# The last three of 256 row gathers, each issued in two parts (2 rows and 126 rows)

## The chip, the core and the metric

One core of a Trainium2 chip runs the whole program. The metric is device time in microseconds (us) of one execution; the kernel before was timed in three runs, and their median counts. Beside it stands one profiled execution, from whose trace all rows here come.

## What is computed

The reference is a chain of transformer blocks on 256 tokens of width 1024 (two layers with feed-forward parts and attention, then convolution mixers and a cross attention). Its last part is what this change touches. For each token, 8 heads choose 16 experts each out of 16384; each chosen expert is a row of `u` and a row of `v`:

```python
u_sel = jnp.take(u, ec, axis=0)
act = gelu(jnp.einsum('chkd,cd->chk', u_sel, hc)) * gc
v_sel = jnp.take(v, ec, axis=0)
return jnp.einsum('chk,chkd->cd', act, v_sel)
```

The result is added to the token's vector, a final RMS norm follows, and the 256 x 1024 output is written.

## The kernel before, in words

The tokens are two tiles (t = 0 and 1) of 128, one token to a partition. A head choice is a column of 128 indices, one per token, so there are 2 x 128 = 256 columns n (`N_ROWS`), gathered in order. `u` and `v` stand side by side in one table, `peer_uv`, so that one gathered row is 2048 floats (8 KB), and one gather of 128 rows is 1 MB.

**POOL** (`gather`, line 786, its DMA at line 806) issues one indirect DMA for each n: row p of the table named by `IDX[p, n]` goes to partition p of `row_pair[n % 16]`. There are 16 such buffers (`ROW_SLOTS`), so from n = 16 on it first waits until the row pair of n - 16 has been used (line 805). The DMA counts `row_loaded[n % 16]` up by 16.

**DVE** (loop from line 2656) does for each n, in this order: `dot(n)` (line 2600: wait for the landing, then product with the token and row sum, into `DOT`); at each fourth n `coefficients` of the four columns before (line 2607: gelu value times gate); and for two of every four columns (n % 4 = 1 or 3) `weighted` (line 2619: coefficient times the v half, added to `XTOK`). It also runs the search for the indices of later heads, whose last step writes 16 columns of `IDX` (line 2580, counted by `idx_ready`). At the end the columns are taken in smaller groups: 252 and 253 together, then 254, then 255 (`COEFS`). The last steps of DVE are thus: dot(252), coefficients of 248 to 251, dot(253), weighted(249), dot(254), weighted(251), coefficients of 252 and 253, dot(255), coefficients of 254, weighted(253), coefficients of 255, weighted(255), `total` (line 2626), `finish` (line 2635).

**ACT** makes the gelu of each group (line 1903) and, for the other two of every four columns (n % 4 = 0 or 2), a diagonal matrix of the coefficients (line 1890). **PE** multiplies that diagonal with the v half (line 1331, two halves of 512 columns, sums kept in PSUM) and ends with a closing product (line 1336); `total` adds PSUM to `XTOK`.

**SP** loads the weights of all earlier parts, then the last gain (line 650), and then waits for the four pieces of the output, `yo_ready`, and writes each (lines 651 to 654): two pieces for token tile 0, two for tile 1.

`mod_ring` is a reused area whose parts hold `IDX`, `DOT`, `CF` and the like in this last stage; the profile shows them all under the name mod_ring.

Of the kernel before, what the change touches and what calls it, by code (L numbers as in the profile page):

```python
# [10 lines left out]
U32 = mybir.dt.uint32  # L11
# [5 lines left out]
P = 128  # L17
# [155 lines left out]
ROW_SLOTS = 16  # L173
# [4 lines left out]
N_ROWS = TT * SLOTS_PER_TILE  # L178
N_HEADS = TT * PH
AHEAD = 3  # L180


def row_use(n):
# [61 lines left out]
def build_program(nc, a, out):  # L245
    ctx = ExitStack()
    with ctx:
# [3 lines left out]
        def sem(name):  # L251
            return ctx.enter_context(nc.semaphore(name))
# [15 lines left out]
        def place(name, at_, n, dt=F32, parts=P):  # L268
            assert at_ + n <= ARENA
            return nc.alloc_sbuf_tensor_at(name, [parts, n], dt, offset=arena_at + 4 * at_)  # L270
# [14 lines left out]
        row_pair = [place(f"row_pair{k}", at_, 2 * D) for k, at_ in enumerate(row_areas)]  # L285
# [112 lines left out]
        def mr(n, a0=None, dt=None):  # L398
            v = mod_ring[:, at_mr[0]:at_mr[0] + n]
            at_mr[0] += n  # L400
            if dt is not None:
                v = v.bitcast(dt)
            return v if a0 is None else v.rearrange("p (a b) -> p a b", a=a0)
# [16 lines left out]
        IDX = mr(256, None, U32)  # L420
# [3 lines left out]
        GS = mr(16)  # L424
        YS = mr(4)
        RT = mr(TT)
        assert at_mr[0] <= 2 * TILE

        ps = ctx.enter_context(nc.psum_tensor("ps", [P, 8, 512], F32))
# [142 lines left out]
        gate_diff = sem("gate_diff")  # L572
        gate_exp = sem("gate_exp")
        idx_ready = sem("idx_ready")
        dots_done = sem("dots_done")
        gelu_ready = sem("gelu_ready")
        cf_ready = sem("cf_ready")
        diag_ready = sem("diag_ready")
        row_loaded = [sem(f"row_loaded{s}") for s in range(ROW_SLOTS)]
# [11 lines left out]
        @block.sync  # L591
        def _(sp):
            sp.dma_start(table[0:NB, :], a["rel_bias"]).then_inc(small_loaded, 16)
            sp.dma_start(onehot[:, :], a["onehot"]).then_inc(small_loaded, 16)
            sp.dma_start(lamp[:, :], a["a_lambda"].partition_broadcast(P).rearrange("q a n -> q (a n)")).then_inc(small_loaded, 16)
            sp.dma_start(fgate_b[:, :], a["fgate_b"]).then_inc(small_loaded, 16)
            sp.dma_start(prm[:, :], a["prm"]).then_inc(prm_loaded, 16)
            sp.dma_start(c_row, a["c_row"].partition_broadcast(P).rearrange("q a n -> q (a n)")).then_inc(c_row_loaded, 16)
            sp.dma_start(X[:, :, :], a["xT"]).then_inc(x_loaded, 16)

            sp.wait_ge(mod_eaten, 2)

            def tiles(name, t0=0, n=None, i=None):

                ln = LIN[name]
                for t in range(t0, t0 + (ln.tiles if n is None else n)):
                    g = ln.tile0 + t
                    if g >= RING:

                        low_wait(sp, g - RING, i)  # L610
                    if name[:2] == "a_" and name != "a_o":
                        sp.dma_start(slot(raw, g), a[name[:3]][int(name[3])]).then_inc(w_loaded[g % RING], 16)
                        continue
                    if name in ("x_k0", "x_k1"):
                        src = a["x_k"][t + 2 * (name == "x_k1")]
                        sp.dma_start(slot(raw, g), src).then_inc(w_loaded[g % RING], 16)
                        continue
                    src = a[name][t] if i is None else a[name][bass.ds(i * BODY + t, 1)].rearrange("a p f -> (a p) f")
                    sp.dma_start(slot(raw, g), src).then_inc(w_loaded[g % RING], 16)

            def ffn(w_in, w_out):
                tiles(w_in, 0, RING)
                with sp.Fori(0, 3) as i:
                    tiles(w_in, RING, BODY, i)
                tiles(w_in, 21, 1)
                tiles(w_out)

            ffn("f00_in", "f00_out")
            for kind, t in A_ORDER:
                tiles(f"a_{kind}{t}")  # L630
            tiles("a_o")
            ffn("f01_in", "f01_out")
            tiles("s_k")
            tiles("s_v")
            ffn("f10_in", "f10_out")
            tiles("b_q")
            tiles("b_o")
            sp.wait_ge(mods_ready, summed(ADA_TILES // 2 - 1))
            sp.dma_start(subk[:, :, :], a["subkT"]).then_inc(sub_loaded, 16)
            sp.dma_start(MEM, a["memT"]).then_inc(mem_loaded, 16)  # L640
            ffn("f11_in", "f11_out")
            for name in ("x_k0", "mix_a", "mix_g", "x_k1", "x_v", "mix_b", "sc_out", "cf_out", "mix_out", "x_q", "x_o"):
                tiles(name)
            tiles("pq", 0, 3)
            sp.wait_ge(units_done, LIN["x_o"].unit_end)
            for t in range(TT):
                sp.dma_start(HTOK[:, t, :], a["norm_peer_row"].partition_broadcast(P).rearrange("q a n -> q (a n)")
                             ).then_inc(gpeer_loaded, 16)
            tiles("pq", 3, 5)
            sp.dma_start(gfin, a["final_norm_g"].partition_broadcast(P).rearrange("q a n -> q (a n)")).then_inc(gfin_loaded, 16)  # L650
            for t in range(TT):
                for c in range(2):
                    sp.wait_ge(yo_ready, 2 * t + c + 1)
                    sp.dma_start(out[t][:, c * 512:(c + 1) * 512], XTOK[:, t, c * 512:(c + 1) * 512]).then_inc(out_written, 16)
            sp.wait_ge(out_written, 32 * TT)
# [3 lines left out]
        def _(pool):  # L659
# [126 lines left out]
            def gather(n):  # L786

                if n % TK == 0:
                    pool.wait_ge(idx_ready, n // TK + 1)
                if n == 1:  # L790
                    pool.wait_ge(el_ready, ESET["attX"] + DC)
                if n == 3:
                    pool.wait_ge(tok_turned, 4)
                if n in (4, 5, 8):

                    pool.wait_ge(low["v"], LOW[pq.tile0 + {4: 5, 5: 6, 8: 7}[n]][1])
                if n in (6, 9, 11):

                    pool.wait_ge(units_done, CHUNK_UNIT[pq.chunk0 + 2 * {6: 5, 9: 6, 11: 7}[n] + 1])
                if n == 14:  # L800

                    pool.wait_ge(sub_scores, TT * PH)
                if n >= ROW_SLOTS:
                    e, used = row_use(n - ROW_SLOTS)
                    pool.wait_ge(rows_used[e], used)
                pool.indirect_dma_start(  # L806
                    out=row_pair[n % ROW_SLOTS][:, :], out_offset=None, in_=a["peer_uv"],
                    in_offset=bass.IndirectOffsetOnAxis(ap=IDX[:, n:n + 1], axis=0),
                ).then_inc(row_loaded[n % ROW_SLOTS], 16)

            for n in range(N_ROWS):
# [529 lines left out]
        def _(act):  # L1341
# [506 lines left out]
            act.wait_ge(sumsq_ready, RANK[N_PEER] + 1)  # L1848
            f(RT, ps_token, ACT.Sqrt, scale=1.0 / D, bias=eps[:, :]).then_inc(token_root, 1)

            def sub_copies(h):

                for t in range(TT):
                    act.wait_ge(sub_scores, 2 * h + t + 1)
                    f(S[t][:, 2 * h:2 * h + 2, :].rearrange("p a n -> p (a n)"), ps[:, SUBKEY_BANK[t], 0:2 * NK],
                      ACT.Copy, scale=RT[:, t:t + 1]).then_inc(s_ready, 1)

# [40 lines left out]

            for g in range(AHEAD):
                gates_exp(g)  # L1900
            for j, (first, last) in enumerate(COEFS):
# [4 lines left out]
                if last == SLOTS_PER_TILE + ROW_SLOTS:  # L1906
                    length(0)
                g = last // TK - 1 + AHEAD
                if last % TK == 0 and g < N_HEADS:
# [5 lines left out]
        def _(dve):  # L1915
# [572 lines left out]
            dve.wait_ge(token_root, 1)  # L2488
            v.reciprocal(RT, RT).then_inc(token_scale, 1)

# [105 lines left out]

            def dot(n):

                dve.wait_ge(row_loaded[n % ROW_SLOTS], 16 * (n // ROW_SLOTS + 1))
                v.scalar_tensor_tensor(row_u(n), row_u(n), 1.0, HTOK[:, n // SLOTS_PER_TILE, :], ALU.mult, ALU.mult,  # L2600
                                       accum_out=DOT[:, n:n + 1]).then_inc(dots_done, 1)

# [37 lines left out]
            splits = iter(range(pq + 3, pq + 8))  # L2640
            for g in range(AHEAD - 1):
                for _ in head_best(0, g):
# [9 lines left out]
            for t in range(TT):  # L2652
                v.scalar_tensor_tensor(HTOK[:, t, :], XTOK[:, t, :], RT[:, t:t + 1], HTOK[:, t, :], ALU.mult, ALU.mult
                                       ).then_inc(htok_ready, 1)
            dve.wait_ge(htok_ready, TT)
            for n in range(N_ROWS):
                head, k = n // TK, n % TK
                if k == 0:
                    later = search(head + AHEAD) if head + AHEAD < N_HEADS else iter(())
                dot(n)  # L2660
                if n == BATCH - 1:
                    for _ in search(AHEAD - 1):
                        pass
# [119 lines left out]
```

## Time and profile before

| | |
|---|---|
| three timed runs | 2128.24, 2128.47, 2130.43 us; median 2128.47 |
| the profiled execution | 2122.55 us, of which 2120.7 us from the first to the last instruction (its span) |
| busy share of the span | PE 84%, DVE 82%, ACT 40%, POOL 26% |
| bytes | 606.26 MB over the span, 270.57 MB of them on the software queue of POOL |
| first and last gather issued | 1452.2 and 2080.8 us from the span's start |

Times in rows are us from the span's start. A row of the timeline gives start, duration, engine, line, operation, operands and, in brackets, the idle time of the engine just before it and what ended it. The DMA share is the mean busy share of the core's 16 DMA engines: one engine busy alone shows as 0.06. PEclk is the granted clock of TensorE as a share of 2.4 GHz.

### The profile page before, as it was taken

What the parts mean: (1) busy time and instruction counts of PE and PEld (TensorE: products, weight loads), DVE (VectorE), ACT (ScalarE), POOL (GpSimd) and SP (SyncE); (2) the same over time, 40 slices, a digit from 0 to 9 for tenths busy, and PEclk for the clock granted to TensorE, in tenths of its full rate; (3) what the DMA queues carried; (4) which work ended last, traced back from release to release, by engine and by line L of the source; (5) the groups of instructions that cost most, each with busy time, mean ns of one, the idle gap of its engine ahead of it and who ended that gap; (6) DMA issues with size and microseconds to landing.
All of it is one profiled execution on the core that took longest, in us unless ns stands there. A gap on an engine that the chain in (4) does not pass through costs nothing.

```text
span 2120.7 us, 30890 instructions
## 1 busy us (share of the span) xinstructions
PE 1780.8 (84%) x11460; PEld 1499.9 (71%) x11460; DVE 1729.6 (82%) x2997; ACT 858.0 (40%) x1336; POOL 559.9 (26%) x487
## 2 busy tenths in 40 slices
PE   5999898999999998899999999999655665554655
PEld 4999798999999987899899999989222222211221
DVE  5888777888988887754689997758999989998877
ACT  3443466544454446644545445554212111111101
POOL 0111002111001113111320002422555554545441
PEclk7999999999999998999999999999888777778677
DMA  7889733688868884254545444428999999999996
GB/s 319 318 312 370 306 121 140 250 317 297 293 247 321 302 328 165 100 200 172 182 166 195 173 177 169 178 100 319 412 422 422 422 423 422 422 423 422 422 423 262
DMA packets 88784, 606.26 MB, mean 286 GB/s; under 512 B 9763, under 2 KB 11059, under 8 KB 21468
## 3 DMA queue, kind: packets, MB, share of 16 engines
q1 hardware_dynamic: 37708, 245.03, 31.6%
q0 software_dynamic: 37040, 270.57, 30.7%
q10 hardware_dynamic: 13920, 89.15, 10.5%
q8 instruction: 69, 1.13, 0.2%
q14 instruction: 47, 0.39, 0.0%
HBM read 601.53 MB, written 3.18 MB: 285 GB/s over the span
## 4 chain that ended last, share of the span: by engine, by line
PE 22%; DVE 18%; DMA 15%; issue 3%; ACT 2%; POOL 1%; DVEq 0%; POOLq 0%; ACTq 0%
DMA row_pair<-in_peer_uv,mod_ring 15%; PE ps L834 12%; DVE row_pair L2600 4%; DVE w_lo L1923 3%; DVE XTOK L2619 3%; PE ps L865 2%; PE ps L1331 2%; DVE work L2370 2%; PE ps L966 2%; DVE SQ L2370 2%; PE ps L967 1%; POOL row_pair L806 1%; PE ps L897 1%; PE ps L1027 0%; ACT w_hi L1353 0%
## 5 line engine op out<-in xcount | busy, mean ns | idle before, releaser
L1923 DVE TENSOR_TENSOR w_lo<-raw,w_hi 128x2048 fp32r<-128x2048 f32 (+1 forms) x248 | 528.2, 2134 | 183.1 <-ACT w_hi L1353 182.4
L1331 PE MATMUL ps<-row_pair,diag 128*128 128x512 f32 x512 | 356.2, 860 | 265.9 <-ACT diag L1890 265.9
L1353 ACT ACTIVATE w_hi<-raw 128x2048 fp32r<-128x2048 f32 (+1 forms) x248 | 440.2, 1776 | 214.5 <-PE ps L834 70.1
L1331 PEld LDWEIGHTS ps<-row_pair,diag 128*128 128x128 f32 x512 | 136.1, 279 | 485.3 <-ACT diag L1890 321.2
L834 PE MATMUL ps<-HH,w_hi 128*128 128x256 f32 x1584 | 443.9, 280 | 0.5 <-DVE w_lo L1923 0.5
L834 PE MATMUL ps<-HH,w_lo 128*128 128x256 f32 x1584 | 442.2, 279 | 0.0
L834 PE MATMUL ps<-HL,w_hi 128*128 128x256 f32 x1584 | 441.1, 278 | 0.0
L806 POOL DMA_INDIRECT row_pair<-in_peer_uv,mod_ring x256 | 329.3, 1286 | 321.6 <-PE ps L1331 220.4
L2600 DVE SCALAR_TENSOR_TENSOR row_pair<-row_pair,HTOK 128x1024 f32<-128x1024 f32 x256 | 311.5, 1218 | 62.6 <-DMA row_pair<-in_peer_uv,mod_ring 60.1
L834 PEld LDWEIGHTS ps<-HL,w_hi 128*128 128x128 f32 x1584 | 297.6, 188 | 0.7 <-issue 0.7
L834 PEld LDWEIGHTS ps<-HH,w_hi 128*128 128x128 f32 x1584 | 296.4, 187 | 2.1 <-DVE w_lo L1923 1.2
L834 PEld LDWEIGHTS ps<-HH,w_lo 128*128 128x128 f32 x1584 | 296.6, 187 | 0.0
L966 PE MATMUL ps<-GUHL,w_hi 128*128 128x512 f32 x704 | 247.2, 395 | 2.1 <-DVE w_lo L1923 2.1
L720 POOL TENSOR_TENSOR GUHL<-work,GUHL 128x256 f32 (+1 forms) x88 | 79.1, 899 | 537.7 <-ACT GUHL L1473 497.1
L1940 DVE SCALAR_TENSOR_TENSOR mod_ring<-mod_ring,mod_acc 128x1024 f32<-128x1024 f32 x144 | 192.7, 1375 | 19.8 <-DMA mod_ring<-in_ada 19.1
L967 PE MATMUL ps<-GUHL,w_lo 128*128 128x256 f32 x704 | 197.4, 280 | 0.0
L1903 ACT ACTIVATE mod_ring<-mod_ring 128x4 f32<-128x4 f32 (+1 forms) x66 | 13.5, 205 | 397.8 <-DVE row_pair L2600 397.8
L834 PE MATMUL ps<-EH,w_hi 128*128 128x256 f32 x560 | 159.6, 285 | 5.6 <-POOL EL L693 2.8
L2619 DVE SCALAR_TENSOR_TENSOR XTOK<-row_pair,mod_ring,XTOK 128x1024 f32<-128x1024 f32 x126 | 161.2, 1279 | 0.0
L834 PE MATMUL ps<-EL,w_hi 128*128 128x256 f32 x560 | 158.9, 284 | 0.0
L834 PE MATMUL ps<-EH,w_lo 128*128 128x256 f32 x560 | 158.0, 282 | 0.0
L966 PEld LDWEIGHTS ps<-GUHL,w_hi 128*128 128x128 f32 x704 | 132.0, 187 | 33.7 <-DVE w_lo L1923 3.1
(338 smaller groups left out, 3004.3 us busy)
## 6 DMA issues: line engine op xcount, KB each, us to landing
raw<-in_f_in SPq DMA_DIRECT2D x88, 1024.0 KB, 4.9
mod_ring<-in_ada ACTq DMA_DIRECT2D x74, 1024.0 KB, 7.2
raw<-in_f_out SPq DMA_DIRECT2D x64, 704.0 KB, 5.5
raw<-in_mix_a SPq DMA_DIRECT2D x16, 1024.0 KB, 4.8
raw<-in_mix_g SPq DMA_DIRECT2D x8, 1024.0 KB, 4.7
raw<-in_pq SPq DMA_DIRECT2D x8, 1024.0 KB, 5.0
first<-in_ada ACTq DMA_DIRECT2D x4, 1024.0 KB, 13.0
raw<-in_a_q SPq DMA_DIRECT2D x4, 1024.0 KB, 5.1
```

What stands on the lines that cost most here:

```text
L720: nc.gpsimd.tensor_tensor(lo, graw[:, j % 2, :], f32(hi), ALU.subtract).then_inc(hidden_lo, 1)
L806: pool.indirect_dma_start(out=row_pair[n % ROW_SLOTS][:, :], out_offset=None, in_=a["peer_uv"], in_offset=bass.IndirectOffsetOnAxis(ap=IDX ...
L834: ins = mm(out_, ops[1] if left else ops[0], ops[0] if left else ops[1], start=(first and k == k0 and n == 0), stop=(last and k == k1 - 1 ...
L966: mm(pair, w[0][:, kk, :], GUHL[:, :, k * SEQ:(k + 1) * SEQ], start=(k == 0), stop=False)
L967: last = mm(ps[:, BANK[q], 0:SEQ], w[1][:, kk, :], GUH[:, k, :], start=False, stop=(k == FC - 1))
L1331: last = mm(ps[:, 2 * t + c, :], diag[:, d, :], row_v(k)[:, c * 512:(c + 1) * 512], start=False, stop=False)
L1353: f(slot(w_hi, g), slot(raw, g), ACT.Copy).then_inc(hi_ready, 1)
L1923: v.tensor_tensor(slot(w_lo, g), slot(raw, g), f32(slot(w_hi, g)), ALU.subtract).then_inc(low["v"], 1)
L1940: ins = v.scalar_tensor_tensor(w[:, j, :], w[:, j, :], 1.0, c_row, ALU.mult, ALU.mult, accum_out=mod_dot[:, n // 2 % 2, m:m + 1])
L2370: ins = v.scalar_tensor_tensor(dst, x, w31, dst, ALU.mult, ALU.add)
L2600: v.scalar_tensor_tensor(row_u(n), row_u(n), 1.0, HTOK[:, n // SLOTS_PER_TILE, :], ALU.mult, ALU.mult, accum_out=DOT[:, n:n + 1]).then_inc ...
L2619: ins = v.scalar_tensor_tensor(y, row_v(n), CF[:, n:n + 1], y, ALU.mult, ALU.add)
```

## The change

The gathers of n = 253, 254 and 255 become two indirect DMAs each, the first for rows 0 and 1, the second for rows 2 to 127. Because an index column is given from partition 0 on, the indices of the second part are first copied down two partitions, into `part_idx`, by a DMA of SP once the last index is there. Each part counts the buffer's semaphore up by 16, and `dot` waits for one 16 more at these three columns. The copy stands in SP's program ahead of the waits for the output.

```diff
+PARTED = 3
+FIRST_PART = 2
+def row_loads(n):
+    return 2 if n >= N_ROWS - PARTED else 1
...
+        part_idx = mr(PARTED, None, U32)
...
+            sp.wait_ge(idx_ready, N_HEADS)
+            sp.dma_start(part_idx[0:P - FIRST_PART, :], IDX[FIRST_PART:P, N_ROWS - PARTED:N_ROWS]).then_inc(part_idx_loaded, 16)
             for t in range(TT):
                 for c in range(2):
                     sp.wait_ge(yo_ready, 2 * t + c + 1)
...
+                whole = row_loads(n) == 1
+                rows = P if whole else FIRST_PART
                 pool.indirect_dma_start(
-                    out=row_pair[n % ROW_SLOTS][:, :], out_offset=None, in_=a["peer_uv"],
-                    in_offset=bass.IndirectOffsetOnAxis(ap=IDX[:, n:n + 1], axis=0),
+                    out=row_pair[n % ROW_SLOTS][0:rows, :], out_offset=None, in_=a["peer_uv"],
+                    in_offset=bass.IndirectOffsetOnAxis(ap=IDX[0:rows, n:n + 1], axis=0),
+                ).then_inc(row_loaded[n % ROW_SLOTS], 16)
+                if whole:
+                    return
+                k = n - (N_ROWS - PARTED)
+                if k == 0:
+                    pool.wait_ge(part_idx_loaded, 16)
+                pool.indirect_dma_start(
+                    out=row_pair[n % ROW_SLOTS][rows:P, :], out_offset=None, in_=a["peer_uv"],
+                    in_offset=bass.IndirectOffsetOnAxis(ap=part_idx[0:P - rows, k:k + 1], axis=0),
                 ).then_inc(row_loaded[n % ROW_SLOTS], 16)
...
-                dve.wait_ge(row_loaded[n % ROW_SLOTS], 16 * (n // ROW_SLOTS + 1))
+                dve.wait_ge(row_loaded[n % ROW_SLOTS], 16 * (n // ROW_SLOTS + row_loads(n)))
```

## Rows read from the trace of the kernel before

**Rows 1.** The chain that ended last, its last DMA piece: start, length, what.

```profile
2079.59 27.11 DMA row_pair<-in_peer_uv,mod_ring
```

**Rows 2.** Windows of the gather stage and its end; columns in the first line.

```profile
core 0: us, PE busy (x) PEld busy (x) DVE busy (x) ACT busy (x) POOL busy (x), PEclk, DMA share, GB/s
2000.00:2050.00 50.00, 28.88 (x40) 11.12 (x40) 37.74 (x60) 4.50 (x15) 22.56 (x20) 0.76 1.01 422
...
2098.00:2099.00 1.00, 1.00 (x3) 0.19 (x1) 1.00 (x3) 0.00 (x0) 0.00 (x0) 1.00 0.57 238
...
2100.00:2100.50 0.50, 0.00 (x0) 0.00 (x0) 0.50 (x2) 0.00 (x0) 0.00 (x0) 1.00 0.12 49
2100.50:2101.00 0.50, 0.00 (x0) 0.00 (x0) 0.07 (x2) 0.20 (x1) 0.00 (x0) 1.00 0.04 16
...
2107.00:2108.00 1.00, 1.00 (x2) 0.34 (x1) 1.00 (x3) 0.00 (x0) 0.00 (x0) 0.50 0.06 25
...
2108.50:2109.00 0.50, 0.50 (x3) 0.14 (x1) 0.50 (x1) 0.00 (x0) 0.00 (x0) 1.00 0.00 0
```

**Rows 3.** DMA packets of 2101.4 to 2108.5: queue: packets, MB, share of 16 engines.

```profile
DMA packets 25, 0.19 MB, mean 27 GB/s; under 512 B 2, under 2 KB 2, under 8 KB 2
...
q0 software_dynamic: 25, 0.19, 6.3%
```

**Rows 4.** Timeline of the last columns, from dot(252) to the total of tile 1.

```profile
2101.80 1.23 DVE L2600 SCALAR_TENSOR_TENSOR row_pair<-row_pair,HTOK 128x1024 f32<-128x1024 f32 x1 [1.23 <-DMA row_pair<-in_peer_uv,mod_ring]
...
2102.95 0.16 DVE L2607 TENSOR_TENSOR mod_ring<-mod_ring 128x4 f32<-128x4 f32 x1
...
2103.59 5.88 PE L1331 MATMUL ps<-row_pair,diag 128*128 128x512 f32 x8 [4.52 <-ACT diag L1890]
2104.26 1.23 DVE L2600 SCALAR_TENSOR_TENSOR row_pair<-row_pair,HTOK 128x1024 f32<-128x1024 f32 x1 [1.15 <-DMA row_pair<-in_peer_uv,mod_ring]
...
2106.72 1.23 DVE L2600 SCALAR_TENSOR_TENSOR row_pair<-row_pair,HTOK 128x1024 f32<-128x1024 f32 x1
...
2109.07 0.15 DVE L2607 TENSOR_TENSOR mod_ring<-mod_ring 128x2 f32<-128x2 f32 x1
2109.18 1.23 DVE L2600 SCALAR_TENSOR_TENSOR row_pair<-row_pair,HTOK 128x1024 f32<-128x1024 f32 x1
2109.26 0.40 ACT L1890 ACTIVATE diag<-ident,mod_ring 128x128 f32<-128x128 f32 x1 [3.53 <-DVE mod_ring L2607]
...
2109.72 3.70 PE L1331 MATMUL ps<-row_pair,diag 128*128 128x512 f32 x8 [0.24 <-ACT diag L1890]
...
2111.80 1.28 DVE L2619 SCALAR_TENSOR_TENSOR XTOK<-row_pair,mod_ring,XTOK 128x1024 f32<-128x1024 f32 x1
...
2113.90 1.22 DVE L2626 TENSOR_TENSOR XTOK<-XTOK,ps 128x1024 f32<-128x1024 f32 x1 [0.82 <-PE ps L1336]
```

**Rows 5.** POOL: all its gathers (ns min/median/max), and gathers 253 and 255.

```profile
L806 POOL DMA_INDIRECT row_pair<-in_peer_uv,mod_ring x256: 934/1249/2792, 1452.2 to 2080.8; - x128
...
2078.35 0.94 POOL L806 DMA_INDIRECT row_pair<-in_peer_uv,mod_ring  x1 [0.31 <-issue]
...
2080.84 0.94 POOL L806 DMA_INDIRECT row_pair<-in_peer_uv,mod_ring  x1 [0.30 <-issue]
```

**Rows 6.** The index writes of DVE and the output DMAs of SP, first and last start.

```profile
L2580 DVE SCALAR_TENSOR_TENSOR mod_ring<-mod_ring x16: 158/161/175, 1451.8 to 1982.7; 128x16 uint32<-128x16 f32 x16
...
L654 SPq DMA_DIRECT2D out<-XTOK x4: 332/338/348, 1851.6 to 2118.3; - x4
```

**Rows 7.** Packet prices: 1.70 to 1.96 us (all small), and 2117 to 2121 (output).

```profile
DMA packets 48, 0.00 MB, mean 4 GB/s; under 512 B 48, under 2 KB 48, under 8 KB 48
...
q1 hardware_dynamic: 48, 0.00, 8.8%
...
q1 hardware_dynamic: 288, 0.52, 33.9%
```

**Rows 8.** PE's group of eight matmuls one before the last three.

```profile
2093.68 5.40 PE L1331 MATMUL ps<-row_pair,diag 128*128 128x512 f32 x8 [4.54 <-ACT diag L1890]
```

More of the change, by code:

```diff
@@ L574, in build_program @@
         idx_ready = sem("idx_ready")
+        part_idx_loaded = sem("part_idx_loaded")
         dots_done = sem("dots_done")
```

## The prediction

> **What bounds the kernel now.** I read the chain of waits first, from its end backwards. Its last long piece is a gather's transfer, 27.11 us from 2079.59, so it lands at 2106.70 [rows 1]; that is the time at which dot(254) begins. What comes after it is compute of the last columns. So the end is set by the row transfers until the last few us.
>
> Next the windows [rows 2]. Through the stage the DMA share is 1.01 at 422 GB/s: all 16 engines are busy, each at 422 / 16 = 26.4 GB/s, which is 0.31 us for a row of 8,192 bytes and 2.48 us for an equal share of 8 of a gather's 128 rows. But the engines don't stop together. The share falls to 0.57 in 2098 to 2099, to 0.12 (two engines) in 2100 to 2100.5, and then stays at 0.06, one engine, with nothing new started after 2108.5. The packets of that tail prove it [rows 3]: from 2101.4 to 2108.5 only 25 packets are left, 2 of them small (completions) and 23 rows, with 6.3% of 16 engines, which is one engine without a gap at 0.31 us a row. Three gathers have 3 x 8 = 24 rows for one engine. So **one engine is three gathers behind**, fifteen are done by about 2100.7, and columns 253, 254 and 255 wait for the lone one.
>
> Last the timeline [rows 4]. dot(252) waited 1.23 us for its landing at 2101.80, dot(253) 1.15 us at 2104.26, one share of 2.48 later. dot(254) and dot(255) start with no idle time shown: DVE needs nearly as long as the transfer. On the other branch PE works from 2103.59 to 2109.47 on the diagonals of columns 248 and 250 (eight matmuls, 5.88 us), idles 0.24, and takes 3.70 us for the eight of 252 and 254. The total at 2113.90 waited for PE. The granted clock explains 5.88 against 3.70: 0.50 (1.2 GHz) in 2107 to 2108, still in the first group, and 1.00 (2.4 GHz) from 2108.5 on [rows 2].
>
> **The parts of the change.**
>
> *Where the rows go.* No row shows a gather of 2 or 126 rows. Whole gathers go in equal shares of 8. Equal shares of 126 can't be on 16 engines; 14 engines with 9 rows are the nearest (9 engines with 14, 7 with 18, and so on down to one with 126). Two rows make one each on two engines. If the lone engine is one of the two that the 14 leave, it has 1 row in place of 8 in each of three gathers, 21 fewer: 21 x 0.31 = 6.5 us off its tail. The others get 3 more, 0.93 us. Bounds for the lone engine: from no row at all (all 7.4 us of its 24 rows gone) to all 128 of each. I take one row per gather, the case nearest to the equal shares that the rows show in which its load changes. The Trainium skill ("DMA: Bandwidth & Descriptors", section "Why a DMA increments its semaphore by 16 and not by 1") says that a DMA runs on the largest number of engines up to 16 that divides its rows, on POOL's path consecutive ones from a cursor that goes round. By that rule the parts take 2 and 14 engines and bring the cursor back to the same place, so the same two engines are spared three times; the sum is the same by it. No run here shows it.
>
> *POOL.* Three gathers become six. Gather 253 starts at 2078.35 and the next follow at 0.94 + 0.30 us [rows 5], so the sixth part is out by 2078.35 + 6 x 1.25 = 2085.9. The earliest engine stops about 2098 and so reaches column 253 about 7.4 us before, 2090.6. Were each part 2.79 us (the longest gather), the sixth would be out at 2096.9; that delays only engines that have several us to spare. Cost 0; nothing stands behind these on POOL.
>
> *SP and the index copy.* The last index is written at 1982.7, and SP's output DMAs were issued from 1851.6 to 2118.3 [rows 6]. The two for token tile 0, ready at 1851.6, now stand behind the wait for the last index and go out 131 us later, still 135 before the last two. Nothing else waits for them, and their 0.52 MB (1.2 us of all engines) lie in the same full DMA stage either way: 0. POOL's new wait asks for a copy issued near 1983; at 2079 it is long there. The copy itself is 126 runs of 12 bytes, 8 or 9 per engine, taken out of the saturated stage, so it delays the lone engine, dot(252) and all behind. Bounds: 48 small packets took 8.8% of 16 x 0.26 us, 7.6 ns each; 256 output packets of 2 KB took 33.9% of 16 x 4 us, 84 ns each [rows 7]. That is 0.07 to 0.76 us; 12 bytes are nearest to the small ones, so +0.07.
>
> *The tail with the lone engine relieved.* Column 252 is whole and still lands at 2101.80. Then three single rows, 0.93: the lone engine lands 255 by 2102.8. The others stop at 2100.7 + 0.93 = 2101.6 and land 0.5 later. So nothing is awaited after dot(252). DVE: coefficients at 2102.95, and dot(253) 0.11 later (as 2109.07 to 2109.18 in [rows 4]), 2103.06 in place of 2104.26: 1.20 earlier. The next coefficients come at 2107.87 in place of 2109.07, the diagonal of 252 is ready about 2108.5. But PE is in its slow group until 2109.47. It then starts at once: 2109.47 + 3.70 = 2113.17 in place of 2113.42. **Gain 0.24 us**, PE's idle time. DVE's own last product would end at 2113.08 - 1.20 = 2111.88, before PE. What is late next is thus PE at 1.2 GHz. An earlier group of eight took 5.40 us [rows 8]; then the gain would be 0.72. The bound is DVE's 1.20.
>
> **Sum.** -0.24 + 0.07 = -0.17 us. The profiled execution took 2122.55 us (span 2120.7 and 1.85 around it), so 2122.4; the median of the timed runs is 5.92 above it, and I carry the difference over: **2128.3 us**. A measurement of this kernel tells about 0.2% (4.26 us) from no change, since the three runs alone spread by 2.19.
>
> **Rivals.**
>
> A. *The lone engine is among the 14.* It gets 9 rows: columns 253, 254 and 255 land 0.31, 0.62 and 0.93 later. dot(254), which began at its landing, moves by 0.60; so do the coefficients, the diagonal and PE's last group. DVE ends at 2113.08 + 0.93 = 2114.0, before PE's 2114.5. With the copy +0.67: 2129.1. For it: no row tells which engine is the lone one. The Trainium skill (the same page, section "Latency and other measured facts") says that engines 7 and 15 are usually slower; a cursor at 0 would spare 0 and 1, and this rival would hold. The trace shows one lone engine, not a pair, and no number, so this rule bears little.
>
> B. *Few engines take the 126 rows* (the rival that ends slower). Place: the landing of column 255. With r rows an engine in each gather an engine that now stops at 2100.7 stops at 2100.7 + (r - 8) x 0.93. It passes today's 2108.7 from r = 17, seven engines or fewer, and costs 4.3 us more from r = 22: 8 + (8.0 + 4.3) / 0.93. With three engines (r = 42) it is 24 us, 2152; with one, 110 - 8 = 102 us, 2230. Against it: whole gathers use all engines.
>
> C. *The parts are dealt as before*, about 8 rows an engine, the last one less: the change does not do what it says. The lone engine keeps its tail, +0.07 to +0.4: 2128.7.
>
> **Chances.** Relieved 0.50, A 0.38, B 0.05, C 0.07. Between the first two the trace can't choose; I put relief ahead because the whole tail sits on one engine, and it matters little: both lie within 0.04%. Within 0.2% are the first, A and C, 0.95 together, less 0.06 for medians of three runs that differ by themselves and for a stage that runs otherwise without the profiler (5.92 us lie between): **same 0.89**. Of the rest, B past r = 22 gives 0.03, scatter 0.04 up and 0.04 down: **slower 0.07, faster 0.04**. Range: from the bound -1.20 to A with the dearest copy, 0.60 + 0.76 = +1.36, widened by half the spread of the runs, 1.1, on either side: 2126.2 to 2130.9.
>
> **What would show it.** Right: after about 2102.5 no DMA work but output; dot(253) idle-free near 2103.1 after a dot(252) that still waits; PE's last two groups without a gap. Wrong: a share of 0.06 that lasts to 2109 or beyond (A or C), a share of 0.2 to 0.5 past 2109 (B). The forecast falls if the slow matmul group is shorter or PE's clock is up earlier, which frees up to 1.20, or if dot(252) itself lands elsewhere.

## The result and the profile after

The changed kernel takes 2136.88 us in the median of six runs (2135.74 to 2138.34), the kernel before 2129.14 us beside it (six runs, 2128.24 to 2130.43). The ratio is 1.0036 with a 95% interval of 1.0025 to 1.0046: **slower by 7.7 us**, outside the forecast range and beyond the 0.2% that the forecast took as the line of a difference.

The profiled execution of the change took 2137.66 us, with a span of 2135.8. It stood 7.7 us behind the profiled execution of before already at the first `dot` (1480.8 and 1473.1), long before anything changed can act. So I compare one stretch of both traces, from the start of dot(244) to the end of the span: 2120.7 - 2081.95 = 38.7 us before, 2135.8 - 2090.08 = 45.7 us after. The two lines of dot(244), before and after:

```profile
2081.95 1.23 DVE L2600 SCALAR_TENSOR_TENSOR row_pair<-row_pair,HTOK 128x1024 f32<-128x1024 f32 x1 [2.22 <-DMA row_pair<-in_peer_uv,mod_ring]
...
2090.08 1.23 DVE L2622 SCALAR_TENSOR_TENSOR row_pair<-row_pair,HTOK 128x1024 f32<-128x1024 f32 x1 [2.21 <-DMA row_pair<-in_peer_uv,mod_ring]
```

The difference, 7.0 us, agrees with the medians. The index copy and the moved output lie ahead of that stretch; run 1 below times them alone.

First the windows of the changed kernel, as in [rows 2] (columns: window, its length, busy us and instructions of PE, PEld, DVE, ACT, POOL, then PEclk, DMA share, GB/s).

```profile
2050.00:2100.00 50.00, 28.83 (x40) 10.94 (x40) 36.91 (x58) 4.50 (x15) 21.43 (x20) 0.73 1.02 415
2100.00:2102.00 2.00, 0.00 (x0) 0.00 (x0) 0.70 (x1) 0.00 (x0) 0.00 (x0) 1.00 0.95 225
...
2110.00:2112.00 2.00, 0.00 (x0) 0.00 (x0) 2.00 (x3) 0.00 (x0) 0.00 (x0) 1.00 0.90 229
2112.00:2114.00 2.00, 0.00 (x0) 0.00 (x0) 0.49 (x2) 0.00 (x0) 0.00 (x0) 0.85 0.34 94
...
2118.00:2120.00 2.00, 1.88 (x3) 0.84 (x4) 0.95 (x1) 0.36 (x2) 0.00 (x0) 0.50 0.06 25
```

The point is in the last two columns. In the windows from 2100 to 2112 the engines are nearly as busy as before (share 0.86 to 0.95, here the first and the last), yet they move 189 to 233 GB/s, about half of 422. A busy share alone would have hidden this. The tail at 0.06, one engine, is still there after 2114.

The packets of that stretch (number, MB, mean rate; then the queue's packets, MB and share of 16 engines) give the price of a row.

```profile
DMA packets 479, 2.81 MB, mean 216 GB/s; under 512 B 136, under 2 KB 136, under 8 KB 136
...
q0 software_dynamic: 479, 2.81, 91.1%
```

This is 2099 to 2112, 13 us. 479 - 136 = 343 rows of 8 KB took 0.911 x 16 x 13 = 189 us of engine time: **0.55 us a row in place of 0.31** [rows 3]. Read one by one in the packed trace, none of these 343 rows took under 0.35 us, on any engine.

The timeline of the changed kernel, the rows that answer to [rows 4] (dot is now line 2622, the diagonal product 1353, the total 2648):

```profile
2097.53 1.23 DVE L2622 SCALAR_TENSOR_TENSOR row_pair<-row_pair,HTOK 128x1024 f32<-128x1024 f32 x1
...
2101.30 1.23 DVE L2622 SCALAR_TENSOR_TENSOR row_pair<-row_pair,HTOK 128x1024 f32<-128x1024 f32 x1 [2.53 <-DMA row_pair<-in_peer_uv,mod_ring]
...
2105.66 1.22 DVE L2622 SCALAR_TENSOR_TENSOR row_pair<-row_pair,HTOK 128x1024 f32<-128x1024 f32 x1 [3.06 <-DMA row_pair<-in_peer_uv,mod_ring]
...
2113.91 1.23 DVE L2622 SCALAR_TENSOR_TENSOR row_pair<-row_pair,HTOK 128x1024 f32<-128x1024 f32 x1 [1.51 <-DMA row_pair<-in_peer_uv,mod_ring]
...
2116.33 1.23 DVE L2622 SCALAR_TENSOR_TENSOR row_pair<-row_pair,HTOK 128x1024 f32<-128x1024 f32 x1 [1.18 <-DMA row_pair<-in_peer_uv,mod_ring]
...
2119.05 1.23 DVE L2622 SCALAR_TENSOR_TENSOR row_pair<-row_pair,HTOK 128x1024 f32<-128x1024 f32 x1 [1.42 <-DMA row_pair<-in_peer_uv,mod_ring]
...
2124.61 1.22 DVE L2622 SCALAR_TENSOR_TENSOR row_pair<-row_pair,HTOK 128x1024 f32<-128x1024 f32 x1 [0.26 <-DMA row_pair<-in_peer_uv,mod_ring]
...
2129.01 1.22 DVE L2648 TENSOR_TENSOR XTOK<-XTOK,ps 128x1024 f32<-128x1024 f32 x1 [0.51 <-PE ps L1358]
```

These are the dots of 247, 248, 249, 251, 252, 253 and 255, and the total. The same two dots before, 247 and 251:

```profile
2089.41 1.23 DVE L2600 SCALAR_TENSOR_TENSOR row_pair<-row_pair,HTOK 128x1024 f32<-128x1024 f32 x1
...
2099.33 1.23 DVE L2600 SCALAR_TENSOR_TENSOR row_pair<-row_pair,HTOK 128x1024 f32<-128x1024 f32 x1
```

The waits in brackets in the changed kernel's rows are the place of the loss, and it has two pieces. From dot(247) to dot(251) it is 2113.91 - 2097.53 = 16.4 us, against 9.9 before (2099.33 - 2089.41): **+6.5 us**, and these are columns that are gathered *whole*. From dot(252) to the end it is 2135.8 - 2116.33 = 19.5 us against 18.9: **+0.6 us**; dot(253) to dot(255) now follow at 2.78 us, nine rows of 0.31, in place of 2.46. The two pieces make the 7.0, within 0.1.

### The profile page after: what moved, and what is told of

The parts are those of the page before. It is cut to its first block, busy times and chain, and to the rows that moved or that the text cites. A ratio compares the mean times of both kernels' runs of the same rounds, so it can differ in the third digit from the quotient of the medians.

```text
span 2135.8 us, 30894 instructions
## 1 busy us (share of the span) xinstructions
PE 1783.4 (83%) x11460; PEld 1504.1 (70%) x11460; DVE 1728.9 (81%) x2997; ACT 858.3 (40%) x1336; POOL 561.3 (26%) x490
## 4 chain that ended last, share of the span: by engine, by line
PE 23%; DVE 17%; DMA 15%; issue 3%; ACT 2%; POOL 1%; POOLq 0%; DVEq 0%; ACTq 0%
DMA row_pair<-in_peer_uv,mod_ring 15%; PE ps L856 13%; DVE row_pair L2622 4%; DVE w_lo L1945 3%; DVE XTOK L2641 3%; PE ps L1353 2%; PE ps L887 2%; PE ps L988 2%; DVE work L2392 2%; DVE SQ L2392 2%; PE ps L989 1%; POOL row_pair L819 1%; PE ps L919 1%; PE ps L1064 0%; PE ps L1049 0%
## 5 line engine op out<-in xcount | busy, mean ns | idle before, releaser
L1353 PE MATMUL ps<-row_pair,diag 128*128 128x512 f32 x512 | 351.9, 851 | 277.5 <-ACT diag L1912 277.5
L856 PE MATMUL ps<-HH,w_hi 128*128 128x256 f32 x1584 | 450.2, 284 | 0.0
L856 PE MATMUL ps<-HL,w_hi 128*128 128x256 f32 x1584 | 446.8, 282 | 0.0
L819 POOL DMA_INDIRECT row_pair<-in_peer_uv,mod_ring x256 | 322.4, 1259 | 328.6 <-PE ps L1353 228.8
```

Source lines behind the costliest of these rows:

```text
L819: pool.indirect_dma_start(out=row_pair[n % ROW_SLOTS][0:rows, :], out_offset=None, in_=a["peer_uv"], in_offset=bass.IndirectOffsetOnAxis(a ...
L856: ins = mm(out_, ops[1] if left else ops[0], ops[0] if left else ops[1], start=(first and k == k0 and n == 0), stop=(last and k == k1 - 1 ...
L1353: last = mm(ps[:, 2 * t + c, :], diag[:, d, :], row_v(k)[:, c * 512:(c + 1) * 512], start=False, stop=False)
```

## The experiments

Theory D: a row of a part costs more, since its rows are dealt to the DMA engines, and over the partitions, otherwise than those of a whole gather. Rivals: L, only the load on the engine that ends last; X, the copy, the moved output, the added DMAs and waits. "Stretch" is dot(244) to the end of the span in the run's own profiled execution (38.7 before, 45.7 with the change).

**1. The copy, the wait and the moved output alone**

```diff
+                if n == N_ROWS - PARTED:
+                    pool.wait_ge(part_idx_loaded, 16)
                 pool.indirect_dma_start(out=row_pair[n % ROW_SLOTS][:, :], ...
```

> Only the index copy of SP, the wait of POOL for it and the moved output DMAs stay; all 256 gathers are whole. Theory D (a row of a part costs more, because its rows are dealt to the DMA engines in another way than those of a whole gather): as before the change, 2129 +- 1.5 us. Theory L (only the load counts: 9 rows in place of 8 on the engine that ends last): 2129 +- 1.5. Theory X (the copy, the moved output, more DMAs and waits): up to 2137 if the copy or the moved output is at fault.

2128.13 us, ratio 0.9997 (0.9986 to 1.0009), stretch 38.7. So the copy, the waits and the output of tile 0 going out late cost nothing that can be seen; the interval leaves room for -3.0 to +1.9 us, so the forecast's +0.07 for the copy is neither confirmed nor refuted.

**2. Two parts per column, but halves of the columns**

```diff
+                for c in range(parts):
+                    pool.indirect_dma_start(
+                        out=row_pair[n % ROW_SLOTS][:, c * w:(c + 1) * w], ..., element_offset=c * w,
```

> The last three gathers are again two DMAs each, with the copy and all waits of the change, but the parts are halves of the columns: 128 rows of 4 KB each, dealt as a whole gather is. Theory D: 2129 +- 1.5 us, a 4 KB packet at about 0.155 us. Theory L: 2129 +- 1.5, no engine has more bytes. Theory X (six DMAs in place of three): 2137.

2129.66 us, ratio 1.0007 (0.9996 to 1.0018), stretch 38.9. Six DMAs with all the waits cost nothing that can be seen either; the rate stayed at 408 GB/s from 2101 to 2107, with a 4 KB packet at 0.17 us (569 in 1.017 x 16 x 6 us) where 0.155 was expected. Theory X falls with these two.

**3 and 4. Parts with an even load**

```diff
-FIRST_PART = 2
+FIRST_PART = 16
```

> The change with a first part of 16 rows and a second of 112: both numbers are multiples of 16, so each engine can have 1 + 7 = 8 rows, as in a whole gather. Theory D: rows of 8 KB at 0.4 to 0.6 us in place of 0.31 while the parts run, the lone engine slowed too, 2132 to 2137 us. Theory L: 2129 +- 1.5, the load is even. Theory X: 2137.

```diff
-FIRST_PART = 2
+FIRST_PART = 64
```

> The change with two equal parts of 64 rows, 4 + 4 rows on each engine. Theory D: rows at 0.45 to 0.62 us while the parts run (by the Trainium skill, SBUF - State Buffer, section on the DMA port swizzle, partitions 0 to 63 reach only 8 of 16 ports, so the dearest of the splits), 2132 to 2138 us. Theory L: 2129 +- 1.5. Theory X: 2137.

16 and 112 rows: 2137.55 us, ratio 1.0049 (1.0032 to 1.0065), stretch 46.7. 64 and 64 rows: 2135.03, ratio 1.0044 (1.0023 to 1.0064), stretch 46.4. Here no engine gets more rows (the dots of 252 to 255 follow at 2.43 to 2.48 us, eight rows), so theory L falls: the load isn't the price. The packets of the second, 2093 to 2105:

```profile
DMA packets 402, 2.64 MB, mean 220 GB/s; under 512 B 80, under 2 KB 80, under 8 KB 80
...
q0 software_dynamic: 402, 2.64, 101.2%
```

322 rows in 1.012 x 16 x 12 = 194 us: 0.60 us a row, twice the price, with every engine busy. Run 3 has the same price (319 rows from 2097 to 2109, share 1.005), so 64 and 64 wasn't the dearest of the splits, against the expectation. 220 GB/s is what the Trainium skill ("SBUF — State Buffer", section "Door 1: The DMA port swizzle") gives as the limit of a transfer that reaches only 8 of 16 ports, about 218 GB/s; it says that partitions 0 to 63 are such a set, and 64 to 127 the other.

**5 and 6. One half of the rows, at two places**

That rule can be tried with equal parts: 64 rows at partitions 0 to 63, and 64 at 32 to 95, which by it reach all ports. Bytes, number of copied indices and number of DMAs are the same; `lo` is 0 in the one and 32 in the other, and there is one part.

```diff
+                lo, rows = (0, 64) if half else (0, P)
...
-                    out=row_pair[n % ROW_SLOTS][rows:P, :], out_offset=None, in_=a["peer_uv"],
...
+                    out=row_pair[n % ROW_SLOTS][lo:lo + rows, :], out_offset=None, in_=a["peer_uv"],
```

> The last three gathers fetch only rows 0 to 63, one part of 64 each, by copied indices; rows 64 to 127 of these three columns are left out (half the bytes). Theory P (the rows slow down where the partitions that 16 engines write at a time lie on half of the SBUF ports): 8 KB rows at about 0.6 us while these parts run. Theory S (any part smaller than the whole is dealt badly): also slow. Theory N (the slow rows come from two parts in one column): 0.31 us.

> As the run with rows 0 to 63, but rows 32 to 95, again one part of 64, so four rows per engine; the other rows of these columns are left out. Theory P: by the Trainium skill (SBUF - State Buffer, section on the DMA port swizzle) these partitions lie on all 16 ports, four on each, so rows stay at 0.31 us, and the end comes 3 to 5 us earlier than with rows 0 to 63. Theory S: slow as there, 0.6 us, the same time. Theory N: 0.31 us in both.

Rows 0 to 63: 2135.94 us, ratio 1.0035 (1.0021 to 1.0048), stretch 44.8. Rows 32 to 95: 2127.99 us, ratio 0.9998 (0.9986 to 1.0009), stretch 38.4. The packets, first of rows 0 to 63 (2105 to 2113):

```profile
DMA packets 192, 1.29 MB, mean 161 GB/s; under 512 B 35, under 2 KB 35, under 8 KB 35
...
q0 software_dynamic: 192, 1.29, 97.6%
```

and of rows 32 to 95 (2099 to 2104):

```profile
DMA packets 303, 2.11 MB, mean 421 GB/s; under 512 B 46, under 2 KB 46, under 8 KB 46
...
q0 software_dynamic: 303, 2.11, 101.2%
```

157 rows at 0.976 x 16 x 8 / 157 = 0.80 us against 257 at 1.012 x 16 x 5 / 257 = 0.315 us. Same size, all 16 engines busy in both; only the partitions differ, and with them the tokens whose rows are fetched. So theory D holds in the form P: **the price hangs on which partitions are written at one time**, since whole gathers write partitions 0 to 63 too, at 0.31 us. A part smaller than the whole isn't slow as such (S falls), and rows are slow without two parts in a column (N falls). The 0.80 is more than the 0.6 that I expected, and 161 GB/s is less than the section's 218: the port rule gives the direction, not the whole price, and no run here tells the rest. The end came 6.4 us earlier with rows 32 to 95 in the stretches and 8.0 in the medians, where 3 to 5 was expected.

The second run shows one thing more: it is what the forecast described, a lone engine with fewer rows at the old price. Its PE rows and the dot of 253:

```profile
2112.90 1.23 DVE L2617 SCALAR_TENSOR_TENSOR row_pair<-row_pair,HTOK 128x1024 f32<-128x1024 f32 x1
...
2113.46 9.56 PE L1348 MATMUL ps<-row_pair,diag 128*128 128x512 f32 x16 [4.45 <-ACT diag L1907]
```

dot(253) waits for nothing, PE's last two groups run without a gap (9.56 us for 16 matmuls, as 5.88 + 3.70 in [rows 4]), and the stretch is shorter by 0.3 us. That is one execution, and the stretches of the runs at the old price lie between 38.7 and 39.0, so the 0.3 is hardly more than their scatter.

**7. The other order**

```diff
-FIRST_PART = 2
+FIRST_PART = 126
```

> The change with the parts the other way round: rows 0 to 125 first, then rows 126 and 127. If the parts go to 14 and then 2 consecutive engines, two other engines are spared (14 and 15 in place of 0 and 1, if the change began at 0). Chance 1 in 7 that the lone engine is one of them: then the landings of columns 253 to 255 follow each other at 0.31 us, and 2133; otherwise at 2.75 to 2.8 us as with the change, and 2135 to 2138. Rows at about 0.55 us while the parts run in either case (theories P and S).

2137.16 us, ratio 1.0034 (1.0019 to 1.0049), stretch 48.9; 318 rows from 2097 to 2110 at 0.922 x 16 x 13 / 318 = 0.60 us. The last dots follow at 2.76 to 2.87 us, so the lone engine had nine rows again. Of the two outcomes it is the likelier one. The stretch is 3.2 us longer than with the change, but the medians are 0.3 apart; whether the order costs anything, these runs don't tell.

**8 and 9. Which engine is the lone one**

```diff
+            for j, w in enumerate((17, 19, 23, ..., 79)):
+                nc.gpsimd.dma_start(probe[j:j + 1, 0:w], ...).then_inc(probed, 16)
```

> The kernel before, with 16 DMAs of a single row behind the last gather on POOL, of 17 to 79 floats (16 different sizes), each of which should go to one engine, the next one each time. Fifteen should run before 2101 us or as they are issued, and the one that meets the lone engine only when its rows are done, near 2109. Its size tells how far the lone engine stands from the cursor. Time as before, 2128 +- 3 us.

A miss that taught something (2126.65 us in one run, stretch 38.8): all 16 single rows ran one after another on one engine, right behind its gather rows, near 2102.5, long before the lone engine was done at 2112.8. The next of these direct DMAs didn't go to the next engine. So the second probe used DMAs of 2 to 15 rows, each with rows of its own size.

```diff
+            for k in range(2, 16):
+                nc.gpsimd.dma_start(probe[0:k, o:o + k + 1], ...).then_inc(probed, 16)
```

> The kernel before with 14 small DMAs behind the last gather on POOL, of 2, 3, ... 15 rows (12 to 64 bytes a row). In the last probe all 16 single rows ran on one engine, so a DMA of k rows may always go to the same first k engines. Then, if the lone engine is number L of 16, the DMAs with more than L rows leave small packets on it that run only after its last row, near 2109 to 2113, and their number is 15 - L: 14 where L is 0 or 1, none where L is 15. If the engines rotate, the number has no such order. Time as before.

The kernel took 2129.77 us in one run, stretch 39.0. What is left to the lone engine after its last row (2115.74 to 2116, the rate in slices of 6.5 ns), all of it on one engine (6.2% of 16):

```profile
GB/s 1 1 1 3 4 1 4 1 5 1 6 1 6 1 7 1 7 1 8 1 9 1 9 1 10 1 0 0 0 0 0 0 0 0 0 0 0 0 0 0
DMA packets 27, 0.00 MB, mean 2 GB/s; under 512 B 27, under 2 KB 27, under 8 KB 27
...
q0 software_dynamic: 27, 0.00, 6.2%
```

Twelve slices stand above 1 GB/s, rising from 3 to 10: packets of 20 to 64 bytes, **12 of the 14 probes**, those of 4 to 15 rows. The other 15 packets, and two more just ahead of the window, are of 4 bytes. By the expected rule L = 15 - 12 = 3. Of these direct DMAs, one of k rows went to the first k engines of the same order each time, and the lone engine is the fourth of them.

That is the deal of direct DMAs; the parts of a gather were dealt otherwise. The packets of the change, read one by one, show a single row of 8 KB followed by eleven packets of 4 bytes three times on one engine (the small ones from 2097.88, 2098.33 and 2099.03) and three times on another (from 2101.75, 2102.45 and 2103.22), and no more of them. So two engines had one row a column, the same two each time, and the lone engine, with nine rows a column, wasn't one of them.

**10 and 11. One column and six**

```diff
-PARTED = 3
+PARTED = 1
```

> The change for the last column only (n = 255). Theory P, with the lone engine never spared: the other engines take 9 x 0.55 = 5 us for the part, in which the lone engine does 10 rows (0.5 us each) in place of 16; it has 24 + 9 rows to do, the other 23 at 0.31: 5.0 + 7.1 = 12.1 us against 32 x 0.309 = 9.9 before, so the stretch from dot(244) to the end grows by about 2 us (38.8 to 41), 2131 +- 2 us. A cost that is fixed however many columns are parted (something that the parts start) would give +7: 2136.

```diff
-PARTED = 3
+PARTED = 6
```

> The change for the last six columns. Theory P: the others take 6 x 9 x 0.55 = 29.7 us, in which the lone engine does 60 rows at 0.5 us; it has 24 + 54, the other 18 at 0.31: 29.7 + 5.6 = 35.3 us against 72 x 0.309 = 22.2 before, +13: 2142 +- 3 us. A fixed cost: 2136.

One column: stretch 41.0 (expected 41), 2129.70 us, ratio 1.0011 (0.9994 to 1.0027). Six: stretch 52.1, +13.4 (expected +13), 2139.77 us, ratio 1.0058 (1.0041 to 1.0076). For one column the medians alone can't tell the +2.1 us from nothing, but their interval ends at +5.7 and so excludes a fixed +7. The stretch grows by 2.3, 7.0 and 13.4 us for one, three and six columns: the cost grows with the columns parted, and no fixed part shows. The six columns' packets, 2094 to 2118:

```profile
DMA packets 945, 5.33 MB, mean 222 GB/s; under 512 B 294, under 2 KB 294, under 8 KB 294
...
q0 software_dynamic: 945, 5.33, 89.9%
```

651 rows at 0.899 x 16 x 24 / 651 = 0.53 us.

## Why the prediction was wrong

**Where the rows go: the failed step.** The forecast took 0.31 us, the price of a row in a whole gather [rows 2, 3], for the rows of the parts, "the others get 3 more, 0.93 us". The deal itself was as forecast: two engines with one row a column, 14 with nine (2.78 us a column on the lone engine; a share of 0.90 is 14.4 engines). But those rows cost 0.55 us. The bounds I set were of the number of rows only; the price had no bound. A rate measured on one form of transfer, 422 GB/s of whole gathers, was carried to another form without asking what made it. Runs 5 and 6 show that partitions decide. The port table of the section cited above would have been a warning that they can, and the forecast didn't weigh it. It would not have given the price: if each of 14 engines has nine rows that follow each other, which no run shows, engines in step meet on no port by that table, and engines at different rows can. That they meet on *ports* in the change itself is argued from runs 3 to 6, not shown apart.

**And the slow rows hit the lone engine too.** The others could have afforded 27 rows at 0.55 (15 us): they end at about 2113 and were ahead. But while they write, the lone engine's rows of the whole columns 248 to 251 slow down with them, to 16.4 / 32 = 0.51 us each, and those are on the path. That is the 6.5 us. The forecast had "Column 252 is whole and still lands at 2101.80", and among its signs of being wrong "if dot(252) itself lands elsewhere", but no price for that: nothing in it joined the engines with each other except by their load.

**Which engine is spared.** Relief had 0.50 and was wrong; rival A (nine rows on the lone engine) was right in its own piece. Its price for the last columns, +0.60, is what dot(252) to the end shows, +0.6. That the same two engines are spared three times, as the forecast worked out by the rule of a cursor that goes round (the Trainium skill, "DMA: Bandwidth & Descriptors", section "Why a DMA increments its semaphore by 16 and not by 1"), agrees with the trace of the change. That the lone engine wasn't one of them was a matter of chance to the forecast (0.50 against 0.38), and it came out the other way. Whether the cursor goes round, no run here shows: the direct DMAs of runs 8 and 9 began at the same engine each time, and the parts, 2 + 14, end where they began. Of engines that lag, the Trainium skill ("DMA: Bandwidth & Descriptors", section "Latency and other measured facts") names 7 and 15 as usually slower; the measured one is the fourth in the order of run 9, and which number it bears no run shows.

**POOL, SP and the copy: right as far as the runs can tell.** Run 1 shows no cost (ratio 0.9997). The two lines of SP in the changed kernel show the order, the copy first and then the output:

```profile
1989.80 0.92 SPq L661 DMA_DIRECT2D mod_ring<-mod_ring  x1
1990.77 142.98 SPq L665 DMA_DIRECT2D out<-XTOK  x4
```

The first and the last of POOL's six parts in the timeline:

```profile
2086.50 0.88 POOL L819 DMA_INDIRECT row_pair<-in_peer_uv,mod_ring  x1 [0.30 <-issue]
...
2093.63 1.05 POOL L828 DMA_INDIRECT row_pair<-in_peer_uv,mod_ring  x1 [0.30 <-issue]
```

From 2086.50 to 2094.68 they took 8.2 us where 7.5 was reckoned. All were out before dot(247), at 2097.53, and before the first rows of the parts, near 2097.6.

**The tail on DVE and PE: right, but not what was run.** For a relieved lone engine the forecast had -0.24 us, PE's idle gap, and at most -1.20. Run 6, with four rows in place of eight at the old price, shows the mechanism (dot(253) without a wait, PE without a gap) and gave -0.3 in one execution. So a relieved lone engine gains little, because PE's slow group of matmuls is next.

**Chances and range.** "Same" had 0.89 and the range ended at 2130.9. The rival that ends slower was there (B, few engines), but with another mechanism; none priced a slower row. Of the 7.0 us in the stretch, 6.5 are a term that the forecast had at nothing.

## What to carry to other kernels

A DMA rate read in a trace belongs to the shape that was traced. Before a transfer is cut by partitions, ask which partitions the engines write at one time, and price the cut by a trace of the cut form; a cut by columns (run 2, 408 GB/s) or a part at partitions 32 to 95 (run 6, 421) kept nearly the full rate here. And when one engine is late, ask what slows it while the others work: here their slow rows slowed its rows too. The share of busy engines doesn't show this; bytes per second beside it do.

## What the runs showed of the hardware

- A gather of 64 rows at partitions 0 to 63 ran its rows at 0.80 us, one of 64 rows at 32 to 95 at 0.315 us, with the same bytes and all 16 engines busy (runs 5 and 6).
- Engines at such rows also slow an engine that is at rows of a whole gather: columns 248 to 251 came 4.1 us apart on average (16.4 / 4) in place of 2.5.
- Of a gather's parts of 2 and 126 rows, the same two engines had one row a column each time and the lone engine nine (packets of the change, 2.78 us a column).
- Direct DMAs from POOL's queue were dealt otherwise: 14 of 2 to 15 rows began at the same engine each time, and 16 single rows all ran on one engine (runs 8 and 9).
